# Forget attention of the decode requests: column quarters of 32 rows, one for each chunk of two heads

## The chip, the cores and the metric

The kernel runs on one core of a Trainium2 chip. The metric is the time in device microseconds (us) from start to end, lower is better. Engines are called as the profile calls them: PE is TensorE, DVE VectorE, ACT ScalarE, POOL GpSimd, SP the sync engine, which here only issues DMAs.

## What is computed

One layer of a decoder over a prompt of 1024 tokens and over 8 requests of 8 new tokens each, which have 1024 past tokens in a paged cache (8 pages of 128 rows). All is float32. The change touches only the forget attention ("FoX") of the requests. It has 8 heads of width 64:

```python
def fox_block(q, qpos, cq, k, v, ck, kpos):
    l = jnp.einsum('bthd,bshd->bhts', q, k).astype(jnp.float32) * HEAD_DIM ** -0.5
    l = l + jnp.transpose(cq, (0, 2, 1))[..., None] - jnp.transpose(ck, (0, 2, 1))[:, :, None, :]
    p = masked_softmax(l, kpos[None, :] <= qpos[:, None])
    return jnp.einsum('bhts,bshd->bthd', p.astype(v.dtype), v)
```

Here s runs over 1024 past tokens and the 8 new ones, and ck and cq are running sums of the log-forget values. The same requests also go through a second attention branch (NSA: compressed, selected and window keys), whose work is interleaved with it.

## The kernel before

The program has three large stages: attention of the prompt, `request_attention` for the 8 requests, and a long trunk of projections and feed-forward products. The change is in the second, which takes 746 to 999 us of the profiled execution, and in a few loads that the first stage starts for it.

**Rounds.** The requests are taken in pairs, so that there are four rounds, n = 0 to 3 (`N_` = 4), and a closing stretch (n = 4) in which only the late work of round 3 is left. A pair has 2 requests x 8 heads x 8 tokens = 128 rows, which fill the 128 partitions. Before the change row r * 64 + h * 8 + t belongs to request r, head h, token t. With 128 channels in one block of the contraction, two heads of width 64 fit in a block: the 512 channels of a key or value row are 4 chunks c of 128, and chunk c holds heads 2c and 2c + 1.

**Scores.** For each page p, `keys` turns the key rows of both requests on PE (4 blocks of 128 x 128 each), ACT copies request 0's out of PSUM to `kT` and DVE request 1's, and `fox_scores` multiplies. `q_fox` holds, for each chunk, 64 columns of which only the 16 of that chunk's two heads are not zero; so a product of request r and chunk c writes 64 partitions, adds its two heads there and zeros for the other six, and the four chunks add up. That is 8 products of 64 columns x 128 keys a page, which alternate between the requests and so between the two halves of PE's columns. `fox_new_scores` does the same for the new tokens' keys (64 columns), once a round after page 3.

**Values.** DVE adds the decay (`neg_c`, one row for each row of scores), ACT takes exponentials, PE turns the probabilities (`pT_fox`), and `fox_values` multiplies for each tile j of 128 keys and each request r the 64 columns of its rows by all 512 channels of the values: 2 products of 512 columns. Of each result row only the 64 channels of its own head are wanted; `forget_outcome` (DVE) scales all 512 columns to `o_fox`, `out_fox` turns its 4 chunks on PE, and `forget_turned` (DVE) copies the wanted parts to `qfT`. In the last product new tokens are added: 2 products with 64 rows of `v_new`.

**Order.** PE's program is written out by hand in `request_attention`. In round n it goes: page 0's keys turned, then for p = 1 to 7 page p's keys turned and page p - 1's scores, with small pieces of round n - 1's NSA work between; the last scores; NSA turns and values; probabilities turned; `fox_values` for tiles 0 to 3; `hidden` (64 products that need nothing of this branch); `fox_values` for tiles 4 to 7 and the new tokens; the compressed and window keys; `out_fox`. In round 3 the values are done after `hidden`, tiles 0 and 1 at once and the rest in the closing stretch, where tiles 4 to 7 come from `late_values`. PSUM results pass through a ring of three banks, in the order of `ring_entries`.

**The queue of SP.** All page loads are issued by SP in a written order, each after the wait that makes its buffer free: keys of pages 4 to 7 (page p once page p - 4 has been turned), selected values of the round before, values of pages 0 to 3, 16 page numbers of the next round loaded into registers, keys 0 to 3 of the next round, the window, values of pages 4 to 7 (once `fox_values` has done tiles 0 to 3), 16 loads of raw NSA rows of the next round (`raw_rows`), and `decay`, the next round's `neg_c`: 128 rows of 4352 bytes in one DMA. The first round's `neg_c`, mask rows and first pages are issued at the end of the prompt's stage. There are four buffers each for key pages and value pages.

**POOL** fills `q_fox` (memset, then 4 copies a round), adds the mask `fox_new` to the last 64 columns of `neg_c` once it has landed, and DVE's `fox_new` logits wait for that.

## Time and profile before

| | us |
|---|---|
| Time, median of 3 runs | 2427.85 |
| Lowest and highest run | 2425.8 and 2431.33 |
| Profiled execution | 2428.4 |
| PE busy in it | 2369.9 (98%) |
| DVE, ACT, POOL busy | 1236.0, 547.6, 834.1 |
| The stage of the requests | 746 to 999 |

A matmul's duration in it is the time from start to end through the array, and starts are closer than that; so the cost of a group of matmuls is read from the start of the group to the start of the next. "Idle before" in brackets is time in which the engine did nothing, with what ended it. A DMA share of 1.00 means 16 DMA engines busy all the time; packets that overlap bring it slightly above.

### The profile page before, as it was taken

To read this page: it belongs to the slowest core of one execution; us is meant where nothing else is said; L and a number is where in the kernel's file an instruction comes from. 1 tells how busy PE (TensorE), PEld (TensorE's weight loads), DVE (VectorE), ACT (ScalarE), POOL (GpSimd) and SP (SyncE) were. 2 spreads that over 40 slices of the span, in tenths; PEclk is the share of its full clock that TensorE was granted. 3 is DMA by queue.
4 is the path that set the end of the run, shared out by engine and by line. 5 is a ranking of instruction groups with operands and counts; after the bars stand their busy time and mean duration, and the time that the engine had idled before them with its cause. 6 is when DMAs were issued, how large, how long until landed. Compare 5 with 4: busy or idle time off the path is not lost.

```text
span 2428.4 us, 30908 instructions
## 1 busy us (share of the span) xinstructions
PE 2369.9 (98%) x10983; PEld 1532.6 (63%) x10983; DVE 1236.0 (51%) x3115; ACT 547.6 (23%) x1328; POOL 834.1 (34%) x874
## 2 busy tenths in 40 slices
PE   8999999999998999999999999999999999999999
PEld 4544665555556777688886458888888874443343
DVE  4876716776773444522322794433334324229765
ACT  0001016666663333111111221111011110001131
POOL 0000004554454000475753453334333227203531
PEclk9999999999999999999999999999999999999999
DMA  5423830021018887632325301111111115543201
GB/s 185 106 82 86 273 113 20 1 81 59 1 57 226 234 232 199 209 87 78 87 73 156 83 31 53 36 36 53 35 46 42 36 48 202 175 143 135 84 18 57
DMA packets 185956, 240.28 MB, mean 99 GB/s; under 512 B 53436, under 2 KB 128834, under 8 KB 184266
## 3 DMA queue, kind: packets, MB, share of 16 engines
q1 hardware_dynamic: 181018, 218.99, 29.4%
q10 hardware_dynamic: 1168, 9.58, 1.3%
q0 software_dynamic: 3616, 9.73, 1.2%
q8 instruction: 89, 1.46, 0.3%
q14 instruction: 65, 0.52, 0.1%
HBM read 216.18 MB, written 37.99 MB: 105 GB/s over the span
## 4 chain that ended last, share of the span: by engine, by line
PE 56%; DVE 2%; ACT 1%; issue 0%; DVEq 0%; ACTq 0%
PE ps L2218 36%; PE ps L2382 11%; PE ps L2271 5%; PE ps L2439 2%; PE ps L2369 1%; DVE xT L153 1%; PE ps L2447 1%; ACT xT L2492 0%; PE ps L2275 0%; DVE arena L2970 0%; ACT arena L2589 0%; DVE stats L2644 0%; PE ps L2314 0%; DVE queries L2973 0%; DVE arena L1364 0%
## 5 line engine op out<-in xcount | busy, mean ns | idle before, releaser
L2218 PE MATMUL ps<-xT,arena 128*128 128x272 f32 x1920 | 472.7, 393 | 1.3 <-DVE arena L1375 1.3
L2218 PEld LDWEIGHTS ps<-xT,arena 128*128 128x128 f32 x1920 | 363.9, 190 | 77.0 <-DVE arena L1375 1.7
L2218 PE MATMUL ps<-queries,arena 128*128 128x272 f32 x1312 | 332.6, 393 | 1.8 <-DVE queries L2785 1.0
L2218 PEld LDWEIGHTS ps<-queries,arena 128*128 128x128 f32 x1312 | 249.6, 190 | 54.1 <-DVE queries L2785 1.4
L236 PE MATMUL ps<-arena,xT 128*128 128x512 f32 (+1 forms) x512 | 198.0, 549 | 2.1 <-DMA arena<-in_w_in 1.3
L1008 POOL TENSOR_SCALAR arena<-arena,gates 128x55 f32<-128x55 f32 (+15 forms) x192 | 123.2, 652 | 176.6 <-DVE arena L907 176.4
L943 ACT ACTIVATE arena<-arena 128x640 f32<-128x640 f32 (+15 forms) x256 | 164.7, 643 | 69.0 <-DVE arena L899 49.1
L236 PEld LDWEIGHTS ps<-arena,xT 128*128 128x128 f32 x512 | 97.7, 191 | 102.0 <-issue 93.0
L2218 PE MATMUL ps<-arena 128*128 128x272 f32 x576 | 148.6, 394 | 0.0
L798 PE MATMUL ps<-ident,arena 128*128 128x128 f32 (+4 forms) x880 | 137.8, 284 | 11.0 <-POOL arena L1008 5.2
L786 PE MATMUL ps<-arena,queries 64*128 64x512 f32 (+11 forms) x704 | 128.8, 465 | 14.2 <-DVE arena L899 11.4
L2382 PE MATMUL ps<-arena 128*128 128x512 f32 x312 | 140.7, 599 | 0.0
L798 PEld LDWEIGHTS ps<-ident,arena 128*128 128x128 f32 (+4 forms) x880 | 91.6, 138 | 68.7 <-POOL arena L1008 30.4
L2382 PE MATMUL ps<-xT,arena 128*128 128x512 f32 x304 | 131.6, 592 | 0.0
L2218 PEld LDWEIGHTS ps<-arena 128*128 128x128 f32 x576 | 109.9, 191 | 23.0 <-issue 0.3
L153 DVE STREAM_TRANSPOSE xT<-arena 32x256 f32<-32x256 f32 x264 | 115.1, 436 | 8.6 <-DMA arena<-in_x_all 4.7
L899 DVE CUSTOM_DVE_ANT_0 arena<-ps,arena 128x55 f32<-128x55 f32 (+15 forms) x192 | 96.1, 538 | 44.3 <-PE ps L786 43.3
L915 DVE COPY xT<-ps 128x512 f32<-128x512 f32 (+11 forms) x176 | 85.2, 484 | 52.0 <-PE ps L798 50.5
L2271 PE MATMUL ps<-arena 128*128 128x512 f32 x256 | 110.3, 593 | 0.0
L3105 POOL TENSOR_TENSOR arena<-arena 128x1088 f32<-128x1088 f32 x22 | 54.2, 2486 | 161.8 <-DVE arena L2800 157.7
L2382 PEld LDWEIGHTS ps<-arena 128*128 128x128 f32 x312 | 57.5, 190 | 81.2 <-issue 78.7
L458 PE MATMUL ps<-xT,queries 128*128 128x363 f32 (+1 forms) x336 | 105.3, 474 | 0.0
(345 smaller groups left out, 3275.8 us busy)
## 6 DMA issues: line engine op xcount, KB each, us to landing
arena<-in_cache_fox_kv SPq DMA_DIRECT2D x72, 256.0 KB, 4.3
arena<-in_w_ffn_down SPq DMA_DIRECT2D x68, 256.0 KB, 3.3
arena<-in_w_in SPq DMA_DIRECT2D x16, 1024.0 KB, 5.3
xT<-in_w_ffn_down SPq DMA_DIRECT2D x64, 256.0 KB, 3.9
xT<-in_cache_fox_kv SPq DMA_DIRECT2D x56, 256.0 KB, 6.2
arena<-in_cache_nsa_kv SPq DMA_DIRECT2D x64, 192.0 KB, 7.8
arena<-in_w_ffn_up SPq DMA_DIRECT2D x11, 1024.0 KB, 5.4
arena<-in_w_ffn_gate SPq DMA_DIRECT2D x11, 1024.0 KB
```

The lines of the kernel that those rows point to most:

```text
L153: ins = nc.vector.transpose(out[q * 32:(q + 1) * 32, :, z * 32:(z + 1) * 32], rows[z * 32:(z + 1) * 32, :].rearrange("p (c w) -> p c w", c ...
L236: mm = pe.matmul(ps[:, bank_of(i, n), 0:b - a], keep.xT[:, c, t0:t0 + m], w_rows[:, c, a:b], start=(c == 0), stop=(c == KD - 1))
L458: mm = pe.matmul(ps[:, first + b, 0:n], query_place(keep, kind, g)[:, c, :], keep.xT[:, c, t0:t0 + n], start=(c == 0), stop=(c == KD - 1))
L786: mm = pe.matmul(scores_at(p, half, s, w), q, keys, start=True, stop=True)
L798: mm = pe.transpose(ps[0:w, turn_bank(p, c, half), x * P:(x + 1) * P], probs_of(p, half, s, w), keep.ident[:])
L899: nc.vector.tensor_tensor_reduce(dst, scores_at(p, half), bias, -1.0, FLOOR, ALU.add, ALU.min, low).then_inc(logits_done, 1)
L915: nc.vector.tensor_copy(turned_of(p)[0:w, t0:t0 + m, 1, p.j, :], ps[0:w, turn_bank(p, c, 1), 0:m * P].rearrange("p (t q) -> p t q", t=m)). ...
L943: nc.scalar.activation(x, x, ACT.Exp, bias=nmax[:, p.n % 4, half, 0:1], scale=-1.0, accum_out=sums[:, p.n % 4, half:half + 1]).then_inc(ex ...
L1008: nc.gpsimd.tensor_scalar(x, x, sums[:, p.n % 4, half:half + 1], gate, ALU.mult, ALU.mult).then_inc(normed, 1)
L2218: mm = pe.matmul(ps[:, first + BANK_OF[z], 0:PIECE], weight[:, j, :], moving[:, j, :], start=(j == 0 and z in (1, 6, 5, 7)), stop=(j == kk ...
L2271: mm = pe.matmul(ps[:, q + n, :], mergedT[:, c, t0:t0 + m], at.w_out[:, c, cols], start=(c == 0), stop=(c == KD - 1))
L2382: mm = pe.matmul(ps[:, (0 if z in (1, 2, 7, 4) else 4) + i, :], left[:, i * P:(i + 1) * P], moving, start=(j == 0 and z in (1, 6, 5, 7)), ...
```

## The change

Rows are laid out anew. Row c * 32 + r * 16 + (h mod 2) * 8 + t now belongs to chunk c = h // 2, request r, head h and token t, so that each chunk of two heads owns one quarter of 32 columns of PE and 32 partitions of PSUM.

- `fox_scores` and `fox_new_scores` have 32 columns for a product instead of 64: `q_fox[:, n % 2, r, c, :]` has request r's 16 columns filled and the other request's 16 zero. The sum that was over four chunks is over the two requests. The number of products stays 8.
- `fox_values` has for each tile four products, one for each chunk, each 32 columns by 256: the chunk's 128 channels of both requests' values, side by side. Half of the result (request r's rows with request r's values) is wanted. The new tokens take 8 products of 128 columns instead of 2 of 512.
- `o_fox` shrinks from 512 to 256 columns, `out_fox` turns 2 blocks instead of 4, `q_fox` is 512 columns in all instead of 1280.
- `neg_c` has to lie in the new order, and so comes in 4 DMAs of 32 rows (two runs of 16) instead of one of 128; the first round's mask rows come in 8 DMAs instead of 2.

```diff
@@ -753,9 +753,10 @@
                 sp.dma_start(ahead.block_no[half, :], io["c_block"]).then_inc(keep.const_in, 16)
-                sp.dma_start(ahead.fox_new[half, 56 + 8 * r:64 + 8 * r], io["c_newmask"]).then_inc(keep.filled_in, 16)
+                for c in range(4):
+                    sp.dma_start(ahead.fox_new[32 * c + 16 * r:32 * c + 16 * r + 16, 56 + 8 * r:64 + 8 * r], io["c_newmask"][0:16]).then_inc(keep.filled_in, 16)
             sp.wait_ge(win_copied, 16 * 26)
-            sp.dma_start(ahead.neg_c, io["neg_rows"][0:P, :]).then_inc(keep.neg_c_in, 16)
+            decay_rows(sp, ahead, io, 0, keep.neg_c_in)
             sp.wait_ge(logits_done, 2 * pair_no(1, LAST_TILE, CMP, 1) + 2)
@@ -1006,8 +1007,8 @@
                     nc.gpsimd.tensor_scalar(x, x, sums[:, p.n % 4, half:half + 1], gate, ALU.mult, ALU.mult).then_inc(normed, 1)
-            pool.wait_ge(keep.filled_in, 32)
-            pool.wait_ge(keep.neg_c_in, 16)
+            pool.wait_ge(keep.filled_in, 128)
+            pool.wait_ge(keep.neg_c_in, 64)
             pool.wait_ge(normed, 2 * NPAIR)
@@ -1280,7 +1281,7 @@
         self.rawT_v = at(4, 8, 64, to=29184)
-        self.o_fox = at(FW)
+        self.o_fox = at(FW)[:, 0:2 * P]
         self.neg_c = at(PAST + 64)
@@ -1291,7 +1292,7 @@
         self.winT, self.p_cmp = at(2, WINDOW), at(64)
-        self.q_fox = at(2, 2, 320)
+        self.q_fox = at(2, 2, 4, 32)
 
@@ -1309,6 +1310,13 @@
         sp.dma_start(at.pages[:, p % 4, r, :], fox_page(io, ids[n, r, p], 0)).then_inc(there[p % 4], 16)
+
+
+def decay_rows(sp, at, io, n, there):
+
+    rows = io["neg_rows"][n * P:(n + 1) * P, :].rearrange("(r c x) k -> c r x k", r=2, c=4)
+    for c in range(4):
+        sp.dma_start(at.neg_c[32 * c:32 * (c + 1), :], rows[c]).then_inc(there, 16)
 
@@ -1447,7 +1455,7 @@
                 sp.wait_ge(fox_logits, 2 * n)
-                sp.dma_start(at.neg_c, io["neg_rows"][n * P:(n + 1) * P, :]).then_inc(neg_c_in, 16)
+                decay_rows(sp, at, io, n, neg_c_in)
 
@@ -1497,7 +1505,7 @@
                         rows = slice(h * HD, (h + 1) * HD)
-                        nc.gpsimd.tensor_copy(at.q_fox[rows, n % 2, r, :].rearrange("p (c x) -> p c x", c=4)[:, :, h * 8:h * 8 + 8],
+                        nc.gpsimd.tensor_copy(at.q_fox[rows, n % 2, r, :, r * 16 + h * 8:r * 16 + h * 8 + 8],
                                               keep.qfT[rows, :, tok]).then_inc(queries_ready, 1)
@@ -1512,7 +1520,7 @@
                 if 0 < n < N_:
-                    pool.wait_ge(neg_c_in, 16 * n + 16)
+                    pool.wait_ge(neg_c_in, 64 * n + 64)
                     nc.gpsimd.tensor_tensor(at.neg_c[:, PAST:PAST + 64], at.neg_c[:, PAST:PAST + 64],
@@ -1571,6 +1579,9 @@
 
+            def heads_of(c):
+                return slice(c * 32, (c + 1) * 32)
+
             def fox_scores(n, p):
@@ -1578,20 +1589,20 @@
                 consumed(n, f"k{p}b")
-                for c in range(4):
-                    for r in range(2):
-                        mm = pe.matmul(ps[r * 64:(r + 1) * 64, F0 + p // 4, (p % 4) * P:(p % 4 + 1) * P],
-                                       at.q_fox[:, n % 2, r, c * 64:(c + 1) * 64], at.kT[:, p % 2, r, c, :],
-                                       start=(c == 0), stop=(c == 3))
+                for r in range(2):
+                    for c in range(4):
+                        mm = pe.matmul(ps[heads_of(c), F0 + p // 4, (p % 4) * P:(p % 4 + 1) * P],
+                                       at.q_fox[:, n % 2, r, c, :], at.kT[:, p % 2, r, c, :],
+                                       start=(r == 0), stop=(r == 1))
                 mm.then_inc(fox_scored, 1)
...
                 b = enter(n, "fox_new")
-                for c in range(4):
-                    for r in range(2):
-                        mm = pe.matmul(ps[r * 64:(r + 1) * 64, b, 0:64], at.q_fox[:, n % 2, r, c * 64:(c + 1) * 64],
-                                       keep.newT[:, c, :], start=(c == 0), stop=(c == 3))
+                for r in range(2):
+                    for c in range(4):
+                        mm = pe.matmul(ps[heads_of(c), b, 0:64], at.q_fox[:, n % 2, r, c, :],
+                                       keep.newT[:, c, :], start=(r == 0), stop=(r == 1))
                 mm.then_inc(ring_filled, 1)
@@ -1634,13 +1645,14 @@
                     v = at.late_values if n == N_ - 1 and j >= 4 else at.values
-                    for r in range(2):
-                        mm = pe.matmul(ps[r * 64:(r + 1) * 64, F0, :], at.pT_fox[:, j, r * 64:(r + 1) * 64], v[:, j % 4, r, :],
-                                       start=(j == 0), stop=False)
+                    for c in range(4):
+                        mm = pe.matmul(ps[heads_of(c), F0, 0:2 * P].rearrange("p (r d) -> p r d", r=2), at.pT_fox[:, j, heads_of(c)],
+                                       v[:, j % 4, :, c * P:(c + 1) * P], start=(j == 0), stop=False)
                     if j == NPAGE - 1:
                         for r in range(2):
-                            mm = pe.matmul(ps[r * 64:(r + 1) * 64, F0, :], at.pT_fox[0:64, 8, r * 64:(r + 1) * 64], keep.v_new[0:64, 0:FW],
-                                           start=False, stop=True)
+                            for c in range(4):
+                                mm = pe.matmul(ps[heads_of(c), F0, r * P:(r + 1) * P], at.pT_fox[0:64, 8, heads_of(c)],
+                                               keep.v_new[0:64, c * P:(c + 1) * P], start=False, stop=(r == 1))
                     if j in (3, NPAGE - 1):
@@ -1706,8 +1718,8 @@
                 b = enter(n, "out_fox")
-                for c in range(4):
-                    mm = turn(b, c * P, P, at.o_fox[:, c * P:(c + 1) * P])
+                for r in range(2):
+                    mm = turn(b, r * P, P, at.o_fox[:, r * P:(r + 1) * P])
                 mm.then_inc(ring_filled, 1)
@@ -1912,7 +1924,7 @@
                 dve.wait_ge(fox_inverse, 2 * n + 2)
-                nc.vector.tensor_scalar(at.o_fox, ps[:, F0, :], fox_inv, None, ALU.mult).then_inc(o_saved, 1)
+                nc.vector.tensor_scalar(at.o_fox, ps[:, F0, 0:2 * P], fox_inv, None, ALU.mult).then_inc(o_saved, 1)
 
@@ -1920,9 +1932,9 @@
                         rows = slice(h * HD, (h + 1) * HD)
-                        columns = bank[rows, b * 512:b * 512 + 4 * 144].rearrange("p (c x) -> p c x", x=144)
+                        columns = ps[rows, b, r * P:(r + 1) * P].rearrange("p (c x) -> p c x", x=32)
                         ins = nc.vector.tensor_copy(keep.qfT[rows, :, T + 16 * n + 8 * r:T + 16 * n + 8 * r + 8],
-                                                    columns[:, :, r * 64 + 8 * h:r * 64 + 8 * h + 8])
+                                                    columns[:, :, r * 16 + 8 * h:r * 16 + 8 * h + 8])
                 ins.then_inc(ring_dve, 1)```

On PE, round 1, from the turning of the last keys' probabilities to the compressed keys (L1564, after the change L1572, is the turning; L1638 and L1642 are `fox_values`, then L1649 and L1654; L1656 is `hidden`). Before:

```order
L1564 MATMUL ps<-ident,xT 64x128
L1638 MATMUL ps<-xT 64x512 x8
L1656 MATMUL ps<-arena 128x252 x32
L1638 MATMUL ps<-xT 64x512 x8
L1642 MATMUL ps<-v_new,xT 64x512 x2
L1666 MATMUL ps<-arena 64x63 x4
```

And with the change:

```order
L1572 MATMUL ps<-ident,xT 64x128
L1649 MATMUL ps<-xT 32x256 x16
L1668 MATMUL ps<-arena 128x252 x32
L1649 MATMUL ps<-xT 32x256 x16
L1654 MATMUL ps<-v_new,xT 32x128 x8
L1678 MATMUL ps<-arena 64x63 x4
```

The first size is the number of partitions written. Nothing moves; each group has twice (the new tokens four times) the products, with half the partitions and half (a quarter of) the columns.

On SP, the end of a round's loads: the last raw rows, the decay, the next round's page 4. Before:

```order
L1320 ISA
L1320 DMA arena<-in_cache_nsa_kv 64x2x384
L1450 DMA arena<-neg_rows 128x1088
L1311 ISA
L1311 DMA arena<-in_cache_fox_kv 128x512
```

And with the change:

```order
L1328 ISA
L1328 DMA arena<-in_cache_nsa_kv 64x2x384
L1319 DMA arena<-neg_rows 32x1x1088 x4
L1312 ISA
L1312 DMA arena<-in_cache_fox_kv 128x512
```

Three DMA issues more stand ahead of the next round's keys; no other row of the queue has another place.

## Rows read from the trace of the kernel before

**Rows 1.** The page: span, and busy time of PE (share, instructions).

```profile
span 2428.4 us, 30908 instructions
...
PE 2369.9 (98%) x10983; PEld 1532.6 (63%) x10983; DVE 1236.0 (51%) x3115; ACT 547.6 (23%) x1328; POOL 834.1 (34%) x874
```

**Rows 2.** Rounds 0 and 1: stretch, length, busy per engine, clock, DMA share, GB/s.

```profile
746.00:803.90 57.90, 52.85 (x415) 39.21 (x414) 17.72 (x38) 17.16 (x29) 20.76 (x51) 0.97 0.97 255
803.90:865.40 61.50, 59.03 (x502) 43.45 (x501) 24.97 (x65) 20.41 (x37) 3.86 (x10) 1.00 0.83 239
```

**Rows 3.** Timeline of PE, round 0: start, length, line, tiles, [idle before].

```profile
747.89 1.09 PE L1583 MATMUL ps<-arena,xT 128*64 128x128 f32 x16 [0.28 <-POOL xT L1500]
748.92 1.09 PE L1564 MATMUL ps<-ident,arena 128*128 128x128 f32 x8
...
752.91 0.64 PE L1593 MATMUL ps<-newT,xT 128*64 128x64 f32 x16
753.47 1.09 PE L1564 MATMUL ps<-ident,arena 128*128 128x128 f32 x8
```

**Rows 4.** Timeline, weight loads of the value products of round 0, by pairs.

```profile
777.10 0.17 PEld L1638 LDWEIGHTS ps<-xT 128*64 128x64 f32 x2 [0.26 <-issue]
...
777.53 0.17 PEld L1638 LDWEIGHTS ps<-xT 128*64 128x64 f32 x2 [0.26 <-issue]
```

**Rows 5.** Timeline of PE around the value products of all rounds.

```profile
797.61 1.08 PE L1642 MATMUL ps<-v_new,xT 64*64 64x512 f32 x4
798.62 0.45 PE L1666 MATMUL ps<-arena 128*64 128x63 f32 x8
...
859.07 1.08 PE L1642 MATMUL ps<-v_new,xT 64*64 64x512 f32 x4
...
920.49 1.07 PE L1642 MATMUL ps<-v_new,xT 64*64 64x512 f32 x4
...
974.71 1.94 PE L1638 MATMUL ps<-xT 128*64 128x512 f32 x8
...
988.35 1.07 PE L1642 MATMUL ps<-v_new,xT 64*64 64x512 f32 x4
990.40 0.66 PE L1564 MATMUL ps<-ident,arena 128*128 128x128 f32 x4 [0.98 <-DVE arena L1915]
```

**Rows 6.** Timeline of PE: the turning of page 4's keys in round 1.

```profile
812.68 1.20 PE L1564 MATMUL ps<-ident,arena 128*128 128x128 f32 x9
```

**Rows 7.** Timeline of PE where round 0's raw rows are turned, and that stretch's clock.

```profile
765.45 4.11 PE L1564 MATMUL ps<-ident,arena 128*128 128x128 f32 x20 [2.71 <-DMA arena<-in_cache_nsa_kv]
...
764.00:768.00 4.00, 2.55 (x12) 2.55 (x13) 0.54 (x1) 1.39 (x3) 4.00 (x9) 0.65 1.07 296
```

**Rows 8.** Timeline of SP's queue, round 1.

```profile
805.42 6.86 SPq L1311 DMA_DIRECT2D arena<-in_cache_fox_kv  x8
812.47 8.99 SPq L1461 DMA_DIRECT2D arena<-in_cache_nsa_kv  x16
...
834.90 3.96 SPq L1311 DMA_DIRECT2D arena<-in_cache_fox_kv  x8
...
858.65 0.59 SPq L1450 DMA_DIRECT2D arena<-neg_rows  x1
866.87 6.83 SPq L1311 DMA_DIRECT2D arena<-in_cache_fox_kv  x8
```

**Rows 9.** DMA issues at 805.9, 867.4, 928.8 us (page 4's keys): us to landing.

```profile
arena<-in_cache_fox_kv SPq DMA_DIRECT2D x1, 256.0 KB, 5.0
...
arena<-in_cache_fox_kv SPq DMA_DIRECT2D x1, 256.0 KB, 4.4
...
arena<-in_cache_fox_kv SPq DMA_DIRECT2D x1, 256.0 KB, 3.9
```

**Rows 10.** DMA issues at 846.3, 907.7, 978.8 us (page 7's values): us to landing.

```profile
xT<-in_cache_fox_kv SPq DMA_DIRECT2D x1, 256.0 KB, 10.2
...
xT<-in_cache_fox_kv SPq DMA_DIRECT2D x1, 256.0 KB, 9.3
...
arena<-in_cache_fox_kv SPq DMA_DIRECT2D x1, 256.0 KB, 7.6
```

**Rows 11.** Busy time and DMA share from values to next keys, columns as Rows 2.

```profile
776.00:808.00 32.00, 31.21 (x190) 20.76 (x191) 6.19 (x21) 6.99 (x13) 2.27 (x12) 1.00 1.07 278
```

## The prediction

> **What bounds the kernel now.** The page comes first: PE is busy for 2369.9 us of a span of 2428.4 [rows 1], so what shortens PE's program counts, unless a wait takes its place. The profiled execution lies 0.6 us above the median of the runs (2427.85); the sum is made against 2428.4 and carried over as a difference. Next, busy time by rounds of the requests' stage [rows 2]: PE 52.85 of 57.90 us and 59.03 of 61.50, but the DMA share is 0.97 and 0.83. So a second bound stands close behind PE here, and most of the working below is about how much of PE's gain it lets through. The timelines of PE and of SP's queue, and the landing times of single DMAs, tell that.
>
> **How fast such products run.** A page's 8 score products are 16 instructions and take from 747.89 to 748.92, 1.03 us [rows 3]. A column costs two cycles of 2.4 GHz in each instruction, so 128 columns stream in 107 ns; one after another 16 would need 1.7 us. They take 1.03 because the two requests' products lie in different halves of PE's columns and run together: 8 steps of 109 ns and some 0.15 us for the change from turning to 64-wide products. The values show the pairs directly: two weight loads at 777.10, two at 777.53 [rows 4], a step of 0.43 us for two streams of 512 columns. No row of the trace has products 32 columns wide. The bounds are: four run together as two do now (the extension of rows 3 and 4), only two do, or none. I take four, since what makes two overlap is that they own different columns of the array, and the change gives each chunk its own quarter.
>
> **The parts on PE, with four together.**
> - Page scores: 16 instructions in 4 steps of 109 ns instead of 8 [rows 3]: 0.43 us less for a page, 32 pages, 13.8 us.
> - New tokens' scores: 752.91 to 753.47 is 0.56 us for 8 steps of 58 ns [rows 3]; four steps fewer, 0.23 us, four times: 0.9 us.
> - Values: a tile is now 2 steps of 0.43 [rows 4]; then 2 steps of 256 columns, 0.22 each. 0.42 less, 32 tiles, 13.5 us (3.4 a round).
> - New tokens' values: 797.61 to 798.62, 1.01 us [rows 5], become 4 steps of 109 ns and the change of form, 0.54: 0.47 a round, 1.9 us.
> - `out_fox`: two turnings of 109 ns fewer (8 of them take 1.02) a round, 0.9 us in all. The DVE step before it halves its columns, which shows only at the end, inside an idle of 0.98 us [rows 5]: 0.3. The first scores wait 0.28 us for POOL to clear `q_fox` [rows 3]; fewer columns end that: 0.3.
>
> Sum: 31.6 us. If none of it were lost, the execution would take 2396.8.
>
> **The parts elsewhere.** DVE and ACT keep their copies. A page's turn on PE shortens from 2.05 to 1.62 us, DVE's copy takes 0.69 and ACT's 0.6 of it, so this cover holds; DVE's busy time in a round is 24.97 of 61.50 [rows 2]. SP issues three DMAs more for each `decay`, at 0.59 us one [rows 8]: 1.8 us. Behind them stand the keys of page 4. SP is free from 859.3 to 866.87, when those keys' wait ends [rows 8], so 7.6 us cover 1.8 even after PE has come some 4 us nearer. The 9 extra DMAs in the prompt's stage stand ahead of a wait of SP's queue that is still far from over there; cost nothing.
>
> **What the loads let through.** From 776 to 808 the DMA share is 1.07 [rows 11]: the engines are full and a load lands when its turn comes, not when PE is ready. Three kinds of load matter.
> - Round 0's raw rows: PE already waits 2.71 us for them, to 765.45 [rows 7]. Eight pages of scores done sooner only lengthen that. They land sooner only as far as SP issues sooner: the last thing ahead of them, the keys of page 7, waits for page 3 to be turned, ahead of which stand two score groups and the POOL wait: 0.28 + 2 x 0.43 = 1.1 us.
> - Values of page 7 in a round: issued at 784.9, 846.3, 907.7, they land 10.2, 10.2, 9.3 us later [rows 10] (the first has the same row as the second), at 795.1, 856.5, 917.0. The value products end at 797.61, 859.07, 920.49 [rows 5]. There are only 2.5 to 3.5 us between.
> - Keys of page 4: landed at 810.9, 871.8, 932.7 [rows 9]. PE begins to turn them at 813.2 (the last four of the nine at 812.68, [rows 6]), and 61.4 later in each next round, as SP's waits repeat (805.42, 866.87, [rows 8]). 2.3 to 3.2 us.
>
> All loads of a round come in one train, which starts with SP's issue of page 7's keys and goes on without a wait for PE: selected values 812.47 to 821.46, values, page numbers, the next keys at 834.90 [rows 8]. So a train comes sooner by as much as page 3 is turned sooner in that round: the gain at the start of the round plus 2 x 0.43.
>
> Walked through (gains in us at each place):
> - Round 0: raw rows +1.1. Values of tiles 0 to 3 +1.7, hidden in nothing: 2.8. Page 7's values land 795.1 - 1.1 = 794.0; with 0.5 for the last tile the products end at 794.5 instead of 797.61: +3.1. New tokens and `out_fox` +0.7: 3.8 at the start of round 1.
> - Round 1: page 4's keys land 810.9 - 1.1 = 809.8 and PE would be there at 807.9; gain 3.4. Five score groups, 5.5. This round's train: 3.8 + 0.9 = 4.6 sooner. Page 7's values land at 851.9, products end 852.4 instead of 859.07: 6.7; then 7.4.
> - Round 2: page 4 at 867.2 instead of 874.6: 7.4; five groups, 9.5; train 8.3 sooner; values land 908.8, end 909.3 instead of 920.49: 11.2; then 11.9.
> - Round 3: page 4 at 924.4 instead of 936.0: 11.6; five groups: 13.8, and it stays so through `hidden` to 974.71.
> - The close: late values are issued when `hidden` ends, so their landing moves with it: 978.8 + 7.6 = 986.4 is 11.7 after 974.71 [rows 5, 10]. The products reached the new tokens 13.6 after it (988.35) and now do 12.2 after it: 1.5. With 0.5, 0.2 and 0.3 of the parts above: 2.5.
>
> Total 16.3 us; the other 15 become waits of PE for loads, seven of 1.5 to 2.3 us and a longer first one. 2428.4 - 16.3 = 2412.1, on the median 2411.6.
>
> The Trainium skill, TensorE: Matmul & The Clock Gate, "Measured speedup vs the span model", gives 2.38 times for three column tiles, not 3. An estimate from that page: four tiles would give 3.2, a page's scores would take 0.55 us in steps instead of 0.44, and PE's parts would sum to some 25 us instead of 31.6; since half of the sum is lost to loads anyway, the time would rise by less, to about 2414. Pairs here run at 1.96 (16 x 107 in 8 x 109), above what that table suggests.
>
> **Rivals.**
> - A. **The loads don't bind.** If page 4's and page 7's loads land sooner than walked through (the train is denser, because its values no longer wait for PE behind the window's loads), up to all of 31.6 us survives: 2397. For it: SP's queue has idle time. Against it: the share of 1.07 [rows 11].
> - B. **PE's clock falls in the new waits.** After the idle of 2.71 us the granted clock is 0.65 in the 4 us from 764 [rows 7], a mix of the levels 1.2 and 2.4 GHz: 4 x 0.35 / 0.5 = 2.8 us at the lower one, in which 1.4 us of work isn't done. If each of the seven new waits brings that, and the next wait for a load hides none of it, 9.8 us go: 2421. For it: the row; against it: the new waits are shorter than 2.71. The same page of the Trainium skill (its Part 1) says that idleness lowers the clock and sustained work restores it; by this rule the time is B's, and the row at 764 agrees that it can happen.
> - C. **Only two 32-wide products run together.** The steps then number as before (scores 8 x 109, a tile 4 x 0.22): only `out_fox`, 0.9, and bits are left, less one more 0.1 us for changes of form here and there: 2426.5. Nothing in the trace excludes it.
> - D. **Slower: 32-wide products run one after another.** Place: lines 1583 and 1638. Scores 16 x 109 instead of 8 x 109 ns, 0.87 x 32 = 28 us more; tiles 8 x 0.22 instead of 0.86, 0.87 x 32 = 28; new tokens 4. About 2485, with loads no bound any more. It decides below two at a time; at exactly two the change is even. Against it: rows 3 and 4.
>
> **How the numbers follow.** Forecast 0.62 (2404 to 2419 on its own, from loads that land 1 us sooner in each round to waits that are half as long again); A 0.10; B 0.12; C 0.10; D 0.06. What a measurement of this kernel can tell from no change is about 0.2%, 5 us. Forecast, A and B are faster by more: 0.84; C is same, and with the tail of B 0.10; slower 0.06. A range from 2400 to 2424 holds the forecast, nearly all of B and half of A, about 0.79 to 0.8.
>
> **What would show each step.** In the new profile: instructions of the scores in steps of four, a page's scores 0.6 us from start to start, `hidden` starting 1.8 instead of 3.6 us after the first value product; PE idle ended by DMA at page 4's keys and page 7's values, 1.5 to 2.3 us each; a raw wait of round 0 of about 4 to 5 us; rounds 1 and 2 of 57 to 58 us instead of 61.5; clock 1.00 in them (B if not). Wrong would make it above all 32-wide products that don't run four together (C, D), and loads whose order or speed changes with their new times (A).

## The result and the profile after

The changed kernel takes 2440.57 us (median of 5 runs, 2436.29 to 2445.89), the kernel before beside it 2428.36. The ratio is 1.0050 (95% interval 1.0033 to 1.0066): 12 us slower, where 16 us faster was forecast.

The page of the kernel after gives its span and PE's busy time (columns as in [rows 1]).

```profile
span 2435.2 us, 31262 instructions
...
PE 2345.2 (96%) x11151; PEld 1520.3 (62%) x11151; DVE 1235.9 (51%) x3115; ACT 546.9 (22%) x1328; POOL 832.4 (34%) x874
```

PE has 24.7 us less to do than in [rows 1], and yet the span is 6.8 us longer. So PE's idle time grew by 31.5 us, from 58.5 to 90.0. The list of who waited for whom (total us, times, longest) names almost all of it:

```profile
PE ps L1572 <- DMA arena<-in_cache_fox_kv: 28.7, 5, 11.3
...
PE ps L1572 <- DMA arena<-in_cache_nsa_kv: 3.6, 1, 3.6
...
PE ps L1649 <- DMA arena<-in_cache_fox_kv: 0.9, 1, 0.9
```

The first and the last are new; the second was 2.7 [rows 7]. Together 30.5 of the 31.5 us.

**The products.** Timeline of PE, round 0 after, against [rows 3 to 5]:

```profile
746.96 0.65 PE L1594 MATMUL ps<-arena,xT 128*32 128x128 f32 x16
747.54 1.09 PE L1572 MATMUL ps<-ident,arena 128*128 128x128 f32 x8
...
775.28 1.93 PE L1649 MATMUL ps<-xT 128*32 128x256 f32 x32 [0.68 <-DVE xT L1897]
777.14 13.87 PE L1668 MATMUL ps<-arena 128*128 128x252 f32 x64
...
792.80 0.64 PE L1654 MATMUL ps<-v_new,xT 64*32 64x128 f32 x16
```

A page's scores take 0.58 us from start to start instead of 1.03, four tiles of values 1.86 instead of some 3.6: four 32-wide products run together. Round 0's new-token product starts at 792.80 instead of 797.61, 4.8 us sooner; 0.9 us of that is there at the first scores already (746.96 instead of 747.89).

**The waits.** The new-token products of the next rounds, and PE's waits at page 4's keys:

```profile
859.44 0.64 PE L1654 MATMUL ps<-v_new,xT 64*32 64x128 f32 x16
...
921.19 0.64 PE L1654 MATMUL ps<-v_new,xT 64*32 64x128 f32 x16
...
993.43 0.64 PE L1654 MATMUL ps<-v_new,xT 64*32 64x128 f32 x16
...
817.84 1.97 PE L1572 MATMUL ps<-ident,arena 128*128 128x128 f32 x8 [11.27 <-DMA arena<-in_cache_fox_kv]
...
879.89 1.97 PE L1572 MATMUL ps<-ident,arena 128*128 128x128 f32 x8 [6.67 <-DMA arena<-in_cache_fox_kv]
...
943.89 1.97 PE L1572 MATMUL ps<-ident,arena 128*128 128x128 f32 x8 [8.92 <-DMA arena<-in_cache_fox_kv]
```

Against [rows 5] the places are 0.4, 0.7 and 5.1 us later: each round gains on its products and loses it, and more, in one wait. 11.27 + 6.67 + 8.92 = 26.9 us.

**What is late there.** Timelines of SP's queue and of POOL: the issue of the second and third decay, and POOL's addition that waits for it. The rows in the fence behind them are from the kernel before, with the issue of its second decay.

```profile
794.25 2.70 SPq L1319 DMA_DIRECT2D arena<-neg_rows  x4
...
860.95 2.68 SPq L1319 DMA_DIRECT2D arena<-neg_rows  x4
...
816.75 0.31 POOL L1524 TENSOR_TENSOR arena<-arena 128x64 f32<-128x64 f32 x1 [37.55 <-DMA arena<-neg_rows]
...
878.78 0.32 POOL L1524 TENSOR_TENSOR arena<-arena 128x64 f32<-128x64 f32 x1 [57.62 <-DMA arena<-neg_rows]
```

```profile
797.30 0.59 SPq L1450 DMA_DIRECT2D arena<-neg_rows  x1
...
809.74 0.31 POOL L1516 TENSOR_TENSOR arena<-arena 128x64 f32<-128x64 f32 x1 [25.69 <-DMA arena<-neg_rows]
...
870.05 0.32 POOL L1516 TENSOR_TENSOR arena<-arena 128x64 f32<-128x64 f32 x1 [54.60 <-DMA arena<-neg_rows]
```

From issue to use it was 809.74 - 797.30 = 12.4 us and 870.05 - 858.65 [rows 8] = 11.4; it is now 22.5 and 17.8. The bytes are the same. Busy time in stretches of 2 us (columns as [rows 2]) shows the DMA engines half idle while PE waits:

```profile
806.00:808.00 2.00, 0.58 (x5) 0.31 (x4) 0.00 (x0) 0.26 (x1) 0.00 (x0) 1.00 0.64 204
808.00:810.00 2.00, 0.00 (x0) 0.00 (x0) 0.00 (x0) 0.00 (x0) 0.00 (x0) 0.59 0.21 74
810.00:812.00 2.00, 0.00 (x0) 0.00 (x0) 0.00 (x0) 0.00 (x0) 0.00 (x0) 0.50 0.75 234
812.00:814.00 2.00, 0.00 (x0) 0.00 (x0) 0.00 (x0) 0.00 (x0) 0.00 (x0) 0.50 0.62 174
814.00:816.00 2.00, 0.00 (x0) 0.00 (x0) 0.00 (x0) 0.00 (x0) 0.00 (x0) 0.50 0.44 136
```

The landing times say why: the trace records each count of a load's semaphore. In the kernel before, the decay's one DMA leaves 16 of them when it lands, in each round, and I read each as one of the 16 engines having done its part. After the change each of the decay's four DMAs leaves one count at its issue and two when it lands, in each round: two engines. Page 4's keys, 2 DMAs on 16 engines, have 32 parts. In round 1, 28 of them had landed by 806.3 and the last four at 816.5 to 817.8, just behind the decay's last landing at 816.6; rounds 2 and 3 have the same gap ahead of the last four (870.8 to 879.0, 933.3 to 943.1). The decay's 128 packets of 4352 bytes came one every 0.225 us on average on each of two engines, 14.4 us for 64 each. Before, up to 56 (round 1) and 91 (round 2) such packets landed in 2 us.

The clock (last column but two) is down to 0.50, the level of 1.2 GHz, within the wait, and some of the work behind each wait is done at that level.

**Theory:** a DMA whose rows come in two runs is carried by two engines, and page 4's keys queue behind it on those two. **Rivals:** that there are four DMAs, or that they have 32 rows; that keys would be late anyway with a faster PE; that the clock is the loss.

### The profile page after: what moved, and what is told of

It is laid out like the page before. It is cut to its first block, busy times and chain, and to the rows that moved or that the text cites. A ratio compares the mean times of both kernels' runs of the same rounds, so it can differ in the third digit from the quotient of the medians.

```text
span 2435.2 us, 31262 instructions
## 1 busy us (share of the span) xinstructions
PE 2345.2 (96%) x11151; PEld 1520.3 (62%) x11151; DVE 1235.9 (51%) x3115; ACT 546.9 (22%) x1328; POOL 832.4 (34%) x874
## 4 chain that ended last, share of the span: by engine, by line
PE 55%; DVE 2%; ACT 1%; issue 0%; DVEq 0%; ACTq 0%
PE ps L2230 36%; PE ps L2394 11%; PE ps L2283 5%; PE ps L2451 2%; PE ps L2381 1%; DVE xT L153 1%; PE ps L2459 1%; ACT xT L2504 0%; PE ps L2287 0%; DVE arena L2982 0%; ACT arena L2601 0%; DVE stats L2656 0%; PE ps L2326 0%; DVE queries L2985 0%; DVE arena L1374 0%
## 5 line engine op out<-in xcount | busy, mean ns | idle before, releaser
L1572 PE MATMUL ps<-ident,arena 128*128 128x128 f32 (+1 forms) x548 | 82.6, 296 | 41.9 <-DMA arena<-in_cache_fox_kv 28.7
## 6 DMA issues: line engine op xcount, KB each, us to landing
arena<-in_cache_fox_kv SPq DMA_DIRECT2D x72, 256.0 KB, 5.0
arena<-in_w_ffn_down SPq DMA_DIRECT2D x68, 256.0 KB, 3.3
xT<-in_w_ffn_down SPq DMA_DIRECT2D x64, 256.0 KB, 3.8
xT<-in_cache_fox_kv SPq DMA_DIRECT2D x56, 256.0 KB, 6.2
```

What stands on the lines that cost most here:

```text
L1572: return pe.transpose(ps[0:rows, b, col:col + kk], src, keep.ident[0:kk, 0:kk])
```

## The experiments

**1 to 4: which property of the decay's load costs.** The change with the past decay terms stored in the new order, so that each pair's 128 rows lie together and come in one DMA:

```diff
-            sp.dma_start(io["neg_past"], past[:]).then_inc(past_stored, 16)
+            turned_past = io["neg_past"].rearrange("(n c r h) k -> n r c h k", n=4, c=4, r=2)
+            for b in range(NREQ):
+                sp.dma_start(turned_past[b // 2, b % 2], past[b * 8:(b + 1) * 8, :]).then_inc(past_stored, 16)
...
-    for c in range(4):
-        sp.dma_start(at.neg_c[32 * c:32 * (c + 1), :], rows[c]).then_inc(there, 16)
+    sp.dma_start(at.neg_c, io["neg_rows"][n * P:(n + 1) * P, :]).then_inc(there, 16)
```

> The change, but the decay rows already stand in the new order in HBM (the 64 past rows are stored in that order by 8 small DMAs in the first stage), so that each decay load is one DMA of 128 rows as before. The output stays complete. Theory 1 (in the change's decay loads every DMA of two runs of 16 rows sits on two of the sixteen DMA engines, and the keys of page 4 wait behind it): page 4's keys land again some 5 us after their issue, round 1 near 806 us instead of 817.8, PE waits for them 0 to 2 us instead of 11.3, 6.7 and 8.9, and the time falls to about 2408 to 2413, my forecast for the change. Theory 2 (the 32-wide products finish the rounds sooner than the loads of a round can come, whatever their form): the waits at page 4 only move to other loads, and the time stays above 2425. Theory 3 (the falls of the clock are what costs): the waits shrink but the time gains less than they do.

Measured: 2419.12 us (2415.11 to 2422.66), ratio to before 0.9955 (0.9942 to 0.9969), 21.4 us less than the change. It is faster than both kernels. Each decay load leaves 16 landings again, and no gap stands ahead of the last parts of page 4's keys.

The kernel before, with nothing of the change but its loads of the decay:

```diff
-                sp.dma_start(at.neg_c, io["neg_rows"][n * P:(n + 1) * P, :]).then_inc(neg_c_in, 16)
+    rows = io["neg_rows"][n * P:(n + 1) * P, :].rearrange("(r c x) k -> c r x k", r=2, c=4)
+    for c in range(4):
+        sp.dma_start(at.neg_c[32 * c:32 * (c + 1), :], rows[c]).then_inc(there, 16)
```

> The kernel before, with the change's decay loads alone: four DMAs of two runs of 16 rows. The rows then lie in the wrong partitions for the old layout, so the decay terms of the requests are wrong; the work is the same. Theory 1: neg_rows needs about 15 us of two engines, lands near 817 to 818 in round 1 instead of 809.6, page 4's keys near 819; PE is there at 813.2 and waits 5 to 6 us in each of rounds 1 to 3: 2428 + 16 = about 2444 (2440 to 2450). Theory 2 and 3: no wait or a small one, 2428 to 2431.

Measured: 2452.48 us, ratio 1.0094 (1.0078 to 1.0109), +23 us, more than I had expected. Timeline of PE:

```profile
822.84 1.54 PE L1571 MATMUL ps<-ident,arena 128*128 128x128 f32 x6 [6.92 <-DMA arena<-in_cache_fox_kv]
...
890.50 1.75 PE L1571 MATMUL ps<-ident,arena 128*128 128x128 f32 x7 [4.97 <-DMA arena<-in_cache_fox_kv]
...
959.11 1.97 PE L1571 MATMUL ps<-ident,arena 128*128 128x128 f32 x8 [5.66 <-DMA arena<-in_cache_fox_kv]
```

These are 17.5 us; PE's busy time rises from 2369.9 to 2375.2, 5.3 us, with the same instructions: the lower clock behind each wait. The kernel before suffers from this load too, without any new product. The two effects nearly add up: -9 to -10 us (the first run) and +23 give +13 to +14, against +12 measured.

Four DMAs of 32 rows that lie together, in the kernel before:

```diff
-                sp.dma_start(at.neg_c, io["neg_rows"][n * P:(n + 1) * P, :]).then_inc(neg_c_in, 16)
+    for c in range(4):
+        sp.dma_start(at.neg_c[32 * c:32 * (c + 1), :], io["neg_rows"][n * P + 32 * c:n * P + 32 * (c + 1), :]).then_inc(there, 16)
```

> The kernel before, with each decay load cut into four DMAs of 32 rows that follow each other in HBM, so one run each; the output stays complete. Theory 1 in the form that the outer dimension of the pattern (two runs) sets how many engines are used: one run of 32 rows is spread as 128 rows are, neg_rows lands near 810, time 2428 +- 3. Theory 1b, that 32 rows are too few to be spread, whatever the runs: as the kernel with two runs, 2440 to 2450. If only the number of DMA issues counted: 3 x 0.6 us on SP in each round, hidden, 2428.

Measured: 2430.37 us, ratio 1.0003 (0.9994 to 1.0012). Four DMAs of 32 rows cost nothing that can be told from noise (3 us at most). Each leaves 16 landings.

The change with each run of 16 rows as a DMA of its own:

```diff
-        sp.dma_start(at.neg_c[32 * c:32 * (c + 1), :], rows[c]).then_inc(there, 16)
+        for r in range(2):
+            sp.dma_start(at.neg_c[32 * c + 16 * r:32 * c + 16 * r + 16, :], rows[c, r]).then_inc(there, 16)
```

> The change, with each decay load in eight DMAs of one run of 16 rows instead of four of two runs; the output stays complete. Theory 1 (outer dimension): a single run is spread over all engines, so as the kernel with sorted rows, plus 7 issues of 0.6 us on SP, hidden behind the wait for page 0: 2408 to 2415. Theory 1b (too few rows): each sits on one or two engines, page 4 waits as in the change, about 2440.

Measured: 2420.92 us (2415.78 to 2424.33), ratio 0.9966 (0.9954 to 0.9977), the first run's time within what the runs can tell. Eight DMAs instead of four, rows and order in memory as in the change, and its loss is gone; each of the eight leaves 16 landings.

**5: the number of runs, by itself.** The kernel before; rounds 1, 2, 3 take their decay's rows in 2, 4 and 8 runs:

```diff
-                sp.dma_start(at.neg_c, io["neg_rows"][n * P:(n + 1) * P, :]).then_inc(neg_c_in, 16)
+                runs = 2 ** n
+                rows = io["neg_rows"][0:2 * P, :].rearrange("(a y x) k -> y a x k", a=runs, y=2)
+                sp.dma_start(at.neg_c, rows[0]).then_inc(neg_c_in, 16)
```

> The kernel before, its decay in one DMA of 128 rows for each pair as before, but the rows are taken from the first 256 in runs with a gap behind each: 2 runs of 64 rows in round 1, 4 runs of 32 in round 2, 8 runs of 16 in round 3. Rounds 1 to 3 add the wrong decay terms. If the number of runs sets on how many of the 16 DMA engines the packets lie: at 0.225 us a packet and 128 packets, two engines need 14.4 us in round 1, four 7.2 us in round 2, eight 3.6 us or, beside the other loads, about 5 us as before in round 3; so the keys of page 4 are late in round 1 alone by some 5 us, by 1 to 3 in round 2, and not at all in round 3. If what counts is that the rows lie in several runs at all, or their length: all three rounds are late alike, or round 3, with the shortest runs, the most.

SP's queue, then POOL, then PE at page 4's keys of rounds 1 and 2:

```profile
796.19 0.65 SPq L1452 DMA_DIRECT2D arena<-neg_rows  x1
...
868.04 0.64 SPq L1452 DMA_DIRECT2D arena<-neg_rows  x1
...
930.85 0.69 SPq L1452 DMA_DIRECT2D arena<-neg_rows  x1
...
819.87 0.31 POOL L1518 TENSOR_TENSOR arena<-arena 128x64 f32<-128x64 f32 x1 [36.33 <-DMA arena<-neg_rows]
...
884.67 0.32 POOL L1518 TENSOR_TENSOR arena<-arena 128x64 f32<-128x64 f32 x1 [60.38 <-DMA arena<-neg_rows]
...
940.53 0.32 POOL L1518 TENSOR_TENSOR arena<-arena 128x64 f32<-128x64 f32 x1 [51.44 <-DMA arena<-neg_rows]
...
820.95 1.97 PE L1566 MATMUL ps<-ident,arena 128*128 128x128 f32 x8 [9.35 <-DMA arena<-in_cache_fox_kv]
...
885.65 1.09 PE L1566 MATMUL ps<-ident,arena 128*128 128x128 f32 x8 [1.62 <-DMA arena<-in_cache_fox_kv]
```

From issue to use: 23.7 us with 2 runs, 16.6 with 4, 9.7 with 8; with rows that lie together 10.6 to 12.4 in the three rounds of the kernel before. The landings are 2, 4 and 8. From the start of its first packet to the end of its last the load took 14.5, 11.1 and 5.1 us; at 0.225 us a packet, 128 packets on 2, 4 and 8 engines would take 14.4, 7.2 and 3.6, so with 4 and 8 other loads on the same engines have a part in it. The rest of issue to use is mostly time before the first packet (8.5, 4.3 and 3.8 us), in which the loads ahead are done. PE waits 9.35 and 1.62 us, and in round 3 not at all. Short runs aren't the harm, few are. One whole run of this kernel took 2441.11 us. The Trainium skill has the rule (DMA: Bandwidth & Descriptors, "Why a DMA increments its semaphore by 16 and not by 1", and its table of rules): the number of engines is the largest up to 16 that divides the outermost dimension of both sides. For 2 x 16 rows onto 32 partitions that is two, for 16 or 32 rows that lie together 16; the counts of landings agree at each shape that was run: 2 for 2 x 16 rows, 2, 4 and 8 for the runs of this kernel, 16 for 16, 32 and 128 rows that lie together.

**6 to 8: what bounds the repaired kernel.** From here on all but the last stand on the first run's kernel. A quarter of the bytes of forget keys and values:

```diff
-        sp.dma_start(at.pages[:, p % 4, r, :], fox_page(io, ids[n, r, p], 0)).then_inc(there[p % 4], 16)
+        sp.dma_start(at.pages[:, p % 4, r, 0:P], fox_page(io, ids[n, r, p], 0)[:, 0:P]).then_inc(there[p % 4], 16)
```

(and the same for the values; then each of the two alone.)

> The kernel with sorted decay rows (f1_sorted_rows, 2419.1 us), with only the first 128 of the 512 columns of each key and value page of the forget cache loaded, so a quarter of those bytes in as many DMAs; the products read old contents for the rest, and the requests' forget outputs are wrong. Theory 4 (the change takes 31.6 us off PE's program as summed, and what f1 keeps of it, 10 to 11 us, is cut by waits for loads): nearly all waits for pages go, the clock stays at 1.00, 2397 to 2402. Theory 5 (PE's sum was wrong, the products or their changes of form cost more than summed): no better than 2410.

> The kernel with the decay stored in the new order; of each forget key page only the first 128 of 512 columns are loaded, the values in full. Scores and all forget outputs are computed from what else is there. With less of both the time was 2405.5 us, with all of both 2419.1. If the loads of a round are one train whose length counts, either half gives back about half: 2412. If the key loads are what is late for PE (page 4's, rows of the timeline), this run gives most of the 13.7 us, 2407, and the values' run little, 2417. If page 7's values are, the other way round: 2417 here. Fewer key bytes also let the values land sooner, as they stand ahead in the same engines, so by the train theory the waits at page 7's values (10.0 us in 8 places with all bytes) go in part here too.

> The kernel with the decay stored in the new order; of each forget value page only the first 128 of 512 columns are loaded, the keys in full. The forget outputs are computed from what else is there. One train whose length counts: 2412. Page 7's values as the limit (10.0 us of waits in 8 places with all bytes): 2407 here, 2417 with less of the keys. Keys of page 4 as the limit: 2417 here. In each case the wait for round 0's raw rows stays, 3.6 us or more, since the values come behind them.

Measured: 2405.52 us, ratio 0.9902 (0.9887 to 0.9916), with both; 2407.50, 0.9919 (0.9903 to 0.9936), with keys alone; 2408.49, 0.9927 (0.9910 to 0.9943), with values alone. Either half gives nearly all. I read it so: it is the train of loads whose length counts, and one half less is enough for PE to bound again. None of my three sets of numbers had that. The pages of the first run and of the run with a quarter of both, span and PE:

```profile
span 2420.9 us, 31257 instructions
...
PE 2346.8 (97%) x11151; PEld 1518.3 (63%) x11151; DVE 1235.4 (51%) x3115; ACT 546.9 (23%) x1328; POOL 832.5 (34%) x874
```

```profile
span 2403.6 us, 31257 instructions
...
PE 2339.0 (97%) x11151; PEld 1515.2 (63%) x11151; DVE 1236.8 (51%) x3115; ACT 547.2 (23%) x1328; POOL 835.4 (35%) x874
```

Same instructions, 7.8 us less busy time, and 64.6 us idle instead of 74.1. (The first run's profiled execution, 2422.66 us, is the slowest of its five.) The waits of PE in the first run:

```profile
PE ps L1649 <- DMA xT<-in_cache_fox_kv: 10.0, 8, 2.1
...
PE ps L1572 <- DMA arena<-in_cache_fox_kv: 3.7, 2, 2.2
PE ps L1572 <- DMA arena<-in_cache_nsa_kv: 3.6, 1, 3.6
...
PE ps L1649 <- DMA arena<-in_cache_fox_kv: 0.9, 1, 0.9
```

**9: is it the clock?** Useless products ahead of the waits for values of pages 6 and 7, in rounds 0 to 2:

```diff
+                    if n < N_ - 1 and j in (6, 7):
+                        for l in range(2 if j == 6 else 4):
+                            pe.matmul(ps[:, F1, 0:4 * CMP_N].rearrange("p (x n) -> p x n", x=4), at.w1[:, 1, l, :],
+                                      at.rawT_v[:, :, l % 8, l // 8:l // 8 + CMP_N], start=True, stop=True)
                     pe.wait_ge(v_in[j % 4], 32 * (2 * n + j // 4 + 1))
```

> f1_sorted_rows with extra products that nobody reads, into a bank that is free there: 2 products of 252 columns before the wait for page 6's values and 4 before page 7's, in rounds 0 to 2 (0.9 and 1.7 us of PE work where it would wait 1.1 and 2.1). Theory 3 (the clock falls because of the waits and its fall costs time by itself, as rival B said): clock 1.00 in rounds 1 and 2, 3 to 5 us less than f1, 2414 to 2416. Rival (the fall of the clock is covered by the next wait, for page 4's keys, which ends when the loads have landed): 2418 to 2421.

Measured: 2422.58 us (2418.18 to 2426.65), ratio 0.9967 (0.9954 to 0.9979): no gain. Rounds 1 and 2 in the first run and in this one (from one round's new-token product to that two rounds on):

```profile
797.50:916.60 119.10, 106.35 (x1086) 79.12 (x1082) 49.07 (x128) 40.55 (x74) 7.72 (x20) 0.97 0.80 237
```

```profile
799.20:914.60 115.40, 108.97 (x1113) 81.71 (x1109) 49.05 (x128) 40.58 (x74) 7.76 (x20) 1.00 0.81 244
```

The clock stays at 1.00 and the two rounds are 3.7 us shorter. But in the run with DMAs of 16 rows, which has the first run's products and fills nothing, these two rounds took 116.8 us (797.00 to 913.80), so most of the 3.7 is no more than the scatter between executions. The stages ahead and behind, whose code is the same, were 2.0 and 3.7 us longer in the filled execution, the mean granted clock over the whole is 0.993 in both, and the medians show nothing. The clock's share in the remaining loss stays open.

**10 and 11: loads issued sooner.** POOL issues the selected values of rounds 1 and 2, and SP loads round 3's page numbers sooner, so that SP comes to values and keys sooner; on the first run's kernel, and on the kernel before:

```diff
+            def selected_values(m):
...
+                pool.wait_ge(nsa_pv, m)
+                for x in range(2 * NPAGE):
+                    pool.dma_start(at.v_slc[:, x // NPAGE, x % NPAGE, :], nsa_page(io, ids[x])[:, 384:512]).then_inc(slc_v_pool, 16)
```

> f1_sorted_rows with SP's chain of issues shortened: the selected values of rounds 1 and 2 are issued by POOL (with their page numbers loaded there), and round 3's page numbers are loaded by SP while it waits for page 0 of round 2. The output stays complete. Theory 6 (the loads bind through SP's chain of issues, which starts a round's train at page 3 and spends 9 us each on selected values and page numbers while the DMA engines stand nearly idle): the trains of rounds 2 and 3 start 9 to 18 us sooner, waits for values of page 7 and keys of page 4 go in rounds 2 and 3, 4 to 8 us less than f1: 2411 to 2415. Rival (the bytes bind): 2418 to 2421.

> The kernel before, with the same two moves as f3_earlier_loads (selected values of rounds 1 and 2 issued by POOL, round 3's page numbers loaded sooner), output complete. PE is the bound there, and it waits for none of these loads: 2426 to 2431 by every theory; faster by more than 3 us would say that the loads bound the kernel before, too.

Measured: 2422.04 us, ratio 0.9964 (0.9950 to 0.9977), and 2433.44, 1.0013 (1.0004 to 1.0022). No gain in either; the second is some 3 us slower than the kernel before. Timeline of PE in the first of the two:

```profile
871.42 1.09 PE L1584 MATMUL ps<-ident,arena 128*128 128x128 f32 x8 [2.84 <-DMA arena<-in_cache_fox_kv]
...
990.12 2.15 PE L2242 MATMUL ps<-queries,arena 128*128 128x272 f32 x4 [5.46 <-PEq L1423]
```

The wait moved from the values to page 4's keys, which can't be issued before page 0 is turned, and a new one of 5.46 us stands at the trunk's first product. That wait is 2.78 us in the second of the two and 0.81 to 0.99 in every trace whose page loads are all issued by SP, so it goes with the loads that POOL issues; by what way is not shown. PE's waits for the forget pages did shrink, from 14.6 us in the first run to 10.7, while that for the raw rows grew from 3.6 to 4.7. So this pair doesn't show that SP's order of issues costs nothing: its gain may have gone into the wait at the trunk.

## Why the prediction was wrong, and where it was right

- **The step that failed** is in "The parts elsewhere": the decay's loads were costed as three more issues on SP, 1.8 us under a cover of 7.6. SP's queue did issue them in 2.7 us and cost nothing. What carries the bytes was not costed: two runs for each DMA bring two engines instead of 16, 10 and 6 us more from issue to use (22.5 for 12.4, 17.8 for 11.4), and page 4's keys behind it, for which PE waits 26.9 us in three rounds. Price in this kernel 21.4 us (first run), 23 by itself in the kernel before. No row showed such a load, so it needed a bound from both sides, and it got none.
- **Four products together** held. By groups of the stage's PE instructions (line, engine, shapes, count, busy us, mean ns), before, and in the run with a quarter of the bytes, where loads and clock hardly disturb them:

```profile
L1583 PE MATMUL ps<-arena,xT 128*64 128x128 f32 x512 | 34.9, 279 | 0.3 <-POOL xT L1500 0.3
L1638 PE MATMUL ps<-xT 128*64 128x512 f32 x112 | 26.0, 599 | 2.1 <-DVE xT L1885 2.1
...
L1642 PE MATMUL ps<-v_new,xT 64*64 64x512 f32 x16 | 4.3, 614 | 0.0
...
L1638 PE MATMUL ps<-arena,xT 128*64 128x512 f32 x16 | 3.9, 605 | 0.0
```

```profile
L1594 PE MATMUL ps<-arena,xT 128*32 128x128 f32 x512 | 20.6, 279 | 0.4 <-DVE arena L1897 0.4
L1649 PE MATMUL ps<-xT 128*32 128x256 f32 x224 | 14.0, 382 | 2.1 <-DVE xT L1897 2.1
...
L1654 PE MATMUL ps<-v_new,xT 64*32 64x128 f32 x64 | 2.6, 275 | 0.0
L1649 PE MATMUL ps<-arena,xT 128*32 128x256 f32 x32 | 2.1, 385 | 0.0
```

  Scores 14.3 us less (13.8 forecast), values 29.9 to 16.1, 13.8 (13.5), new tokens' values 1.7 (1.9). PE's busy time falls by 2369.9 - 2339.0 = 30.9 us of the 31.6. Rounds 1 and 2 take 53.7 us each there instead of 61.5 and 61.4, 7.7 less, which is what the sum's parts give for a round. C and D are out.

  By the prediction's estimate from the Trainium skill (TensorE: Matmul & The Clock Gate, "Measured speedup vs the span model") a page's scores would take 0.55 us and the change of form, some 0.7 in all; the measured 0.58 holds both, so four overlap better here than that table for three would have it.
- **What the loads let through** was sized well, once the decay is out of the way. In the first run PE's idle time is 15.6 us more than before, and waits for loads explain 10.0 + 3.7 + 0.9 for the forget pages and 0.9 more for the raw rows, 15.5 of it; the walk had the 15 us. Their place differs: nine waits at values, and two at keys, of which one (1.57 us) is at page 4, instead of seven alternating. The walk's own terms are off by 0.1 in places (1.5 for 13.6 - 12.2 at the close), which changes nothing.
- **Rival B** probably took the rest there. The first run ends 7.5 us below before by its spans (10 by the medians), not 16.3, since PE's busy time fell by 23.1 us, not by 31. The same products took 7.8 us less in the run that hardly waits. In the requests' stage the granted clock was at 0.50 for 24 us in the first run, 7 in the run with a quarter of the bytes, 3 in the kernel before. So some 8 us of lower clock go with these waits, near B's 9.8. That filling the waits didn't bring it back is against taking all of it for B's loss.
- **Rival A** held at one place: in round 0 of the kernel after, page 7's values didn't make PE wait, and from the first scores to the new-token product the round was 3.9 us shorter where 3.1 was forecast at that point. In the first run they did make it wait, 1.55 us. I can't say why they differ there.
- The raw rows' wait of round 0 was forecast at 4 to 5 us; it was 3.6, and 5.4 with fewer bytes.

## What to carry to other kernels

When a new layout of rows changes how a load walks through memory, cost the load anew, even at the same bytes: look at how many pieces its outermost dimension has, and at what waits behind it on the same engines. If it is a small number, store the rows in the order in which they are read, or issue one DMA for each run. And where PE stands close ahead of its loads, a PE saving is worth what the train of loads lets through, less the clock that the new waits cost.

## What the runs showed that was not expected

- The decay took 17.8 to 23.7 us from issue to use in DMAs of two runs of rows, where one DMA of the same bytes in rows that lie together took 10.6 to 12.4. PE waited 11.27 us for what stood behind it in round 1, and over that wait the DMA share was 0.50, 0.21 at its lowest.
- Its harm is to others: in round 1 the keys of pages 4 to 7, loads of 256 KB each, landed 8.9 us after their issue (median of eight) instead of 4.0, and page 4's last part 17.6 us after the page's first issue (800.19 to 817.80), since their parts lie on all engines, those two among them.
- Four 32-wide products in four quarters of PE's columns ran at the pace of one: 16 instructions of 128 columns in 0.58 us, with the change of form, against 1.03 for two 64-wide ones at a time.
- Loading a quarter of the keys alone, or of the values alone, brought 11.6 and 10.6 us, and both together 13.6 (against 2419.12). It looks as if a bound by a train of loads ends at once when the train is shorter than PE's work, wherever it is cut.
